# Hybrid decoder trunk on one core: final norm rebuilt on token rows, and four reordered waits

## The reference

```python
for i in range(DEPTH):                      # i = 0: rglru, i = 1: mlstm
    xn = rms_norm(x, norm_mix[i])
    y, *states = mixer(xn, ...)
    x = x + y
    x = x + swiglu(rms_norm(x, norm_ffn[i]), ffn_w_up[i], ffn_w_down[i])
    gate = jax.nn.sigmoid(x @ ple_w_gate[i] + ple_b_gate[i])
    x = x + gate * (p[i] @ ple_w_proj[i])
y = rms_norm(x, norm_final)                 # returned with all new states
```

## Time and profile before

| | |
|---|---|
| three runs, median | 1933.7 us (1928.45, 1933.7, 1937.48) |
| the profiled execution | 1932.01 us, its span 1930.3 us |
| mean granted TensorE clock | 0.991 |
| PE / ACT / DVE / POOL busy | 98% / 38% / 39% / 40% of the span |

### The profile page before, as it was taken

The page is one execution under the profiler, slowest core; times in us unless marked ns, Lnnn a source line. Parts: engine busy times, 40 slices in busy tenths (PEclk is TensorE's granted clock), DMA queues, the critical chain, the costliest instruction groups (busy, mean ns, idle before and its releaser), DMA issues.

```text
span 1930.3 us, 35958 instructions
## 1 busy us (share of the span) xinstructions
PE 1886.2 (98%) x13703; PEld 1751.1 (91%) x13703; DVE 745.5 (39%) x868; ACT 724.4 (38%) x1062; POOL 780.7 (40%) x663
## 2 busy tenths in 40 slices
PE   7999999999999999999999999999999999999997
PEld 7999999999999999998555555999999999999997
DVE  6677632111111122597766667122231111101214
ACT  4576733322222234444433342423443322212342
POOL 3233554444554544464110101544535545545441
PEclk9999999999999999999999999999999999999998
DMA  4222232222222222322489778232322222222222
GB/s 127 82 83 79 86 100 72 82 88 82 82 82 82 82 82 78 94 77 88 160 262 303 238 246 293 77 93 66 97 79 82 82 82 82 82 82 76 88 80 68
DMA packets 187147, 209.70 MB, mean 109 GB/s; under 512 B 24475, under 2 KB 150051, under 8 KB 186991
## 3 DMA queue, kind: packets, MB, share of 16 engines
q1 hardware_dynamic: 186818, 208.19, 34.9%
q10 hardware_dynamic: 224, 0.07, 0.0%
HBM read 167.57 MB, written 40.64 MB: 108 GB/s over the span
## 4 chain that ended last, share of the span: by engine, by line
PE 87%; DVE 4%; issue 4%; DMA 2%; POOL 2%; ACT 2%; SPq 0%; DVEq 0%; POOLq 0%; ACTq 0%
PE ps L2207 73%; PE ps L2455 2%; PE ps L2553 2%; PE ps L2516 2%; POOL W_LO L662 1%; PE ps L2494 1%; DMA out_ml_C_s_dram<-C_HALVES 1%; PE ps L2389 1%; PE ps L2504 1%; PE ps L2573 1%; DVE H_PAD L1687 1%; PE ps L2378 0%; PE ps L2449 0%; DMA X_ROWS<-in_x_prompt_dram 0%; PE ps L2400 0%
## 5 line engine op out<-in xcount | busy, mean ns | idle before, releaser
L662 POOL TENSOR_TENSOR W_LO<-W_RAW,W_HI 128x512 fp32r<-128x512 f32 x464 | 628.6, 1364 | 731.4 <-ACT W_HI L963 663.8
L963 ACT ACTIVATE W_HI<-W_RAW 128x512 fp32r<-128x512 f32 x484 | 298.5, 628 | 711.6 <-PE ps L2207 707.4
L2207 PE MATMUL ps<-A_HI,W_HI 128*128 128x288 f32 x2304 | 496.3, 297 | 13.1 <-DVE A_LO L1522 4.8
L2207 PE MATMUL ps<-A_LO,W_HI 128*128 128x288 f32 x2304 | 494.7, 296 | 0.0
L2207 PE MATMUL ps<-A_HI,W_LO 128*128 128x288 f32 x2304 | 494.5, 296 | 0.0
L2207 PEld LDWEIGHTS ps<-A_HI,W_HI 128*128 128x128 f32 x2304 | 372.3, 189 | 15.4 <-issue 13.2
L2207 PEld LDWEIGHTS ps<-A_LO,W_HI 128*128 128x128 f32 x2304 | 372.7, 189 | 0.0
L2207 PEld LDWEIGHTS ps<-A_HI,W_LO 128*128 128x128 f32 x2304 | 372.6, 189 | 0.0
L1769 DVE TENSOR_TENSOR X<-X,ps 128x1152 f32 (+1 forms) x36 | 48.7, 1354 | 312.4 <-PE ps L2207 312.4
L2207 PE MATMUL ps<-G_HI,W_HI 128*128 128x288 f32 x768 | 164.6, 296 | 0.5 <-DVEq L1795 0.5
L2207 PE MATMUL ps<-G_HI,W_LO 128*128 128x288 f32 x768 | 164.5, 296 | 0.0
(11 more groups left out here) (383 smaller groups left out, 2248.2 us busy)
## 6 DMA issues: line engine op xcount, KB each, us to landing
W_RAW<-in_ffn_w_up_dram SPq DMA_DIRECT2D x176, 256.0 KB, 2.8
C_HALVES<-in_state_mlstm_C_dram SPq DMA_DIRECT2D x64, 512.0 KB, 5.0
out_ml_C_s_dram<-C_HALVES SPq DMA_DIRECT2D x64, 512.0 KB, 5.3
W_RAW<-in_ffn_w_down_dram SPq DMA_DIRECT2D x88, 256.0 KB, 2.6
W_RAW<-in_ml_w_in_dram SPq DMA_DIRECT2D x64, 256.0 KB, 2.8
W_RAW<-in_rg_w_in_dram SPq DMA_DIRECT2D x48, 256.0 KB, 2.7
W_RAW<-in_ple_w_gate_dram SPq DMA_DIRECT2D x32, 256.0 KB, 2.6
W_RAW<-in_ml_w_out_dram SPq DMA_DIRECT2D x32, 256.0 KB, 2.8
```

The lines of the kernel that those rows point to most:

```text
L662: pool.tensor_tensor(W_LO[:, s], W_RAW[:, s], W_HI[:, s].bitcast(F32), ALU.subtract).then_inc(lo_ready, 1)
L963: act.activation(W_HI[:, s], W_RAW[:, s], ACT.Copy).then_inc(hi_ready, 1)
L2207: ins = pe.matmul(ps[:, 4 * s + 2 * m + h, 0:HALF_T], a[:, w, k, wc], x[:, h * HALF_T:h * HALF_T + HALF_T], start=i == 0 and k == 0 and q ...
```

## The change

1. DVE makes the first two low splits of block 1 ahead of the lambda polynomial.
2. In the first PLE, ACT makes three W_HI splits, the gate, then the fourth split.
3. In the first slab behind the heads, PE runs the passes with W_HI for the whole slab (16 matmuls) once W_HI is there, then waits for W_LO and runs the other 8 (`hi_first`).
4. `states()` puts the two N transposes with the 12 of the RG states into set 0 (bank 3), so two copies-out and two frees are left of four.
5. The end. X_GAIN and the sums of squares over features go. X of the first six chunks is turned into token rows between slabs 0, 1 and 2 of the last job (16 + 14 transposes, banks 4 to 7); DVE multiplies them with a gain row into Y_ROWS, and ACT squares them with a sum along the row. Behind the last slab, chunk 7 comes as X and as gate product, both turned by matmuls with the identity that add up in PSUM, and chunk 6 by transposes; five sums on ACT, a total, root and reciprocal, then DVE and ACT scale Y_ROWS in place (DVE tiles 1, 3 and halves of 0 and 4; ACT tile 2 and the other halves), and SP stores each tile when it is ready. Y_ROWS has a place for each of the five tiles.
6. SP loads the gain row, broadcast to 128 partitions (512 KB), behind the P rows of layer 1; the gain's small load at the start goes.

```diff
@@ sync: behind load_p(1, ...)
+            for half in range(2):
+                sp.wait_ge(cp_stored[half], 16 * HEADS)
+            sp.dma_start(GAIN_ROW[:, :], I["norm_final"].rearrange("(o d) -> o d", o=1).broadcast_to([P, D_MODEL])).then_inc(gain_loaded, 16)
             ffn(1)
...
-                sp.wait_ge(out_rows, i + 1)
+                sp.wait_ge(y_tile[i], 2 if i in (0, 4) else 1)
@@ scalar: ple
-                        for k in range(4):
+                        for k in range(3):
                             split_hi()
                         act.wait_ge(slab_used, jobs.adv(4) + 2 * RING)
...
+                            ins = gate(s, c, C_PB + 2 * m + c + 4 * j)
                         ins.then_inc(psum_freed[s], 1)
...
+                        split_hi()
+                        prep(4 * j + 2 * m, gain, dst)
@@ scalar: last_ple
+            def tile_sum(piece, i, src):
+                n, k = TOKEN_TILES[i][1], sums_t.adv()
+                if k > 2:
+                    act.wait_ge(tile_sums, k - 2)
+                act.activation(SQUARES[0:n, k % 2, 0:src.shape[-1]], src, ACT.Square, accum_out=ROW_SUMS[0:n, piece, i:i + 1]).then_inc(tile_sums, 1)
...
+                    if m == 3:
+                        for i in range(4):
+                            act.wait_ge(gained, i + 1)
+                            tile_sum(0, i, ps[:, 4 + i, :])
+                        act.wait_ge(gained, 5)
+                        tile_sum(0, 4, ps[0:N_STOK, 4, :])
+                        for i, (t0, n) in enumerate(TOKEN_TILES):
+                            act.wait_ge(gained, 6 + i // 2)
+                            tile_sum(1, i, ps[0:n, 5 + i // 2, i % 2 * 2 * P:i % 2 * 2 * P + 2 * P])
+                    act.wait_ge(slab_used, jobs.adv(4) + 2 * RING)
...
+                act.activation(RSTD_COLS[:, 7:8], EPS_COL[:, :], ACT.Sqrt)
+                for i, (t0, n) in enumerate(TOKEN_TILES):
+                    act.wait_ge(turned, 3 + i)
+                    tile_sum(2, i, ps[0:n, LAST_BANKS[i], 0:2 * P])
+                act.wait_ge(total_ready, 1)
+                act.activation(RSTD_COLS[:, 0:5], ROW_TOTAL, ACT.Sqrt, bias=EPS_COL[:, :], scale=1.0 / D_MODEL).then_inc(last_root, 1)
+                act.wait_ge(last_rstd, 1)
+                for i, c0 in ((0, 4 * P), (2, 0), (4, 4 * P)):
+                    n = TOKEN_TILES[i][1]
+                    act.wait_ge(gained, 9 + i)
+                    act.activation(Y_ROWS[0:n, i, c0:], Y_ROWS[0:n, i, c0:], ACT.Copy, scale=RSTD_COLS[0:n, i:i + 1]).then_inc(y_tile[i], 1)
@@ vector
             rg_xc_lo(0)
+            rg_lo(1, 0)
+            rg_lo(1, 1)
             dve.wait_ge(lam_e, 1)
...
-            rg_lo(1, 0)
-            rg_lo(1, 1)
             rg_gate(0, 8)
@@ vector: last_ple, behind the gate of the last pair
+                dve.wait_ge(last_gate, 1)
+                link(dve.tensor_tensor(GATE[:, 0, :], GATE[:, 0, :], P_PROJ[:, 6, :], ALU.mult))
+                dve.wait_ge(last_gate, 2)
+                dve.tensor_tensor(GATE[:, 1, :], GATE[:, 1, :], P_PROJ[:, 7, :], ALU.mult).then_inc(last_gated, 1)
+                dve.tensor_tensor(X[:, 6, :], X[:, 6, :], GATE[:, 0, :], ALU.add).then_inc(xf_ready, 1)
...
+                def late_gain(i):
+                    n = TOKEN_TILES[i][1]
+                    dve.wait_ge(tile_sums, 11 + i)
+                    dve.tensor_tensor(Y_ROWS[0:n, i, EARLY:], ps[0:n, LAST_BANKS[i], 0:2 * P], GAIN_ROW[0:n, EARLY:], ALU.mult).then_inc(gained, 1)
+                for i in range(4):
+                    late_gain(i)
+                dve.wait_ge(tile_sums, 15)
+                dve.tensor_tensor(ROW_TOTAL, ROW_TOTAL, ROW_SUMS[:, 2, :], ALU.add).then_inc(total_ready, 1)
+                late_gain(4)
+                dve.wait_ge(last_root, 1)
+                dve.reciprocal(RSTD_COLS[:, 0:5], RSTD_COLS[:, 0:5]).then_inc(last_rstd, 1)
+                dve.wait_ge(last_rstd, 1)
+                dve.wait_ge(gained, 13)
+                for i, c1 in ((0, 4 * P), (1, 8 * P), (3, 8 * P), (4, 4 * P)):
+                    n = TOKEN_TILES[i][1]
+                    dve.tensor_scalar(Y_ROWS[0:n, i, 0:c1], Y_ROWS[0:n, i, 0:c1], RSTD_COLS[0:n, i:i + 1], None, ALU.mult).then_inc(y_tile[i], 1)
@@ tensor: job
+                    if hi_first and i == 0:
+                        n = slabs.adv()
+                        pe.wait_ge(hi_ready, n + DVE_SLABS)
+                        for part in range(2):
+                            if part:
+                                pe.wait_ge(lo_ready, n + RING)
+                            for k, m, h in itertools.product(range(2), range(2), range(2)):
...
+                                if part:
+                                    ins = pe.matmul(dst, W_LO[:, w, k, wc], hi[:, tokens], start=False, stop=False)
+                                else:
+                                    pe.matmul(dst, W_HI[:, w, k, wc], hi[:, tokens], start=k == 0, stop=False)
+                                    pe.matmul(dst, W_HI[:, w, k, wc], lo[:, tokens], start=False, stop=False)
@@ tensor: states
                 use(0)
...
+                pe.transpose(ps[:, 3, 0:P], N_SAMPLES[:, :, :, :].rearrange("p b h k -> p (b h k)"), IDENT[:, :])
+                pe.transpose(ps[0:16, 3, P:2 * P], N_PROMPT[:, :, :].rearrange("p h k -> p (h k)"), IDENT[:, :]).then_inc(misc_done, 1)
                 use(1)
@@ tensor: last_ple
+                def between(i):
+                    if i == 1:
+                        use(1)
+                        pe.wait_ge(xf_ready, 2)
+                        for t in range(4):
+                            for c in range(4):
+                                ins = turn_out(t, c, 4 + t, c * P)
+                        ins.then_inc(turned, 1)
+                    if i == 2:
+                        pe.wait_ge(xf_ready, 3)
+                        pe.wait_ge(tile_sums, 1)
+                        for c in range(4):
+                            turn_out(4, c, 4, c * P)
+                        for t in range(5):
+                            if t % 2 == 0:
+                                pe.wait_ge(tile_sums, 2 + t // 2)
+                            for c in range(2):
+                                ins = turn_out(t, 4 + c, 5 + t // 2, t % 2 * 2 * P + c * P)
+                        ins.then_inc(turned, 1)
+                job(0, 4, chunks(hi, lo), between)
...
+                pe.wait_ge(tile_sums, 10)
+                pe.wait_ge(gained, 8)
+                for i in range(5):
+                    if i == 4:
+                        pe.wait_ge(last_gate, 1)
+                    add_columns(i, X[:, 7, :], True)
+                pe.wait_ge(last_gated, 1)
+                for i in range(5):
+                    add_columns(i, GATE[:, 1, :], False)
+                pe.wait_ge(xf_ready, 4)
+                for i in range(5):
+                    turn_out(i, 6, LAST_BANKS[i], 0).then_inc(turned, 1)
```

More of the change, by code:

```diff
@@ L786, in ple, with last_ple @@
                 next_norm()
-                for j in (range(2) if last else (None,)):
-                    if last:
-                        body(j)
-                    else:
-                        with loop(pool, 2, {slabs: 8}) as j:
-                            body(j)
+                with loop(pool, 2, {slabs: 8}) as j:
+                    body(j)
+            def last_ple():
+                for k in range(4 + 16):
+                    split_lo()
             def body(j):
@@ L2185, in use, with job @@
                     pe.wait_ge(psum_freed[s], before)
-            def job(s, pairs, operand, before=None, first=0, last=None, own=False):
+            def job(s, pairs, operand, before=None, first=0, last=None, own=False, hi_first=False):
                 if first == 0:
@@ L2311, in ffn @@
                     y_done[0] += ks
-            def turn_out(i):
-                (t0, n), s = TOKEN_TILES[i], i % 2
-                use(s)
-                for c in range(CX):
-                    ins = pe.transpose(ps[0:n, 4 * s + c // 4, (c % 4) * P:(c % 4) * P + P], X_GAIN[:, c, t0:t0 + n], IDENT[:, :])
-                ins.then_inc(misc_done, 1)
             def turn_in(layer):
@@ new lines, in last_ple, with add_columns @@
+            def last_ple(P_HI, P_LO, hi, lo, xn0):
+                project(1, P_HI, P_LO)
+                for m in range(3):
+                    job((m + 1) % 2, 4, chunks(hi, lo), lambda i: pe.wait_ge(xn_ready, xn0 + i + 1))
+                def between(i):
[14 more added lines that the diff above has]
+                                pe.wait_ge(tile_sums, 2 + t // 2)
+                            for c in range(2):
+                                ins = turn_out(t, 4 + c, 5 + t // 2, t % 2 * 2 * P + c * P)
+                        ins.then_inc(turned, 1)
+                job(0, 4, chunks(hi, lo), between)
+                def add_columns(i, src, first):
+                    t0, n = TOKEN_TILES[i]
```

(3 more changed lines are left out.)

214 lines of the change are left out of this document (106 added, 108 removed).

## The result

| | before | after |
|---|---|---|
| median, runs on the same chip | 1934.8 us (10 runs, 1928.45 to 1939.18) | 1917.5 us (10 runs, 1915.48 to 1922.8) |
| ratio, 95% interval | | 0.9915, 0.9901 to 0.9928 |
| profiled execution, its span | 1932.0, 1930.3 us | 1917.9, 1916.2 us |
| mean granted clock | 0.991 | 0.994 |

The kernel became faster by 0.85%. The two traces are 14.1 us apart, the medians 17.4.

The account below looks back on a forecast made before the run. TensorE, busy 98% of the span, was taken as the bound. Gains 2.3 + 0.5 + 3.3 + 2.25 + 4.7 = 13.05 us gave 1918.9 for the profiled execution, 1920.6 against the median; range 1914 to 1927.

Parts of the forecast that it names:

- clock behind the gate: Behind the first PLE's gate, granted clock 0.57 over 4 us; its return, 1.7 us, counted only in a rival of chance 0.16.
- Part 1: Near 50 us, two low splits ahead of the lambda chain end PE's wait: gain 2.3 us, range 1.3 to 2.3.
- Part 2: First PLE: the gate ahead of the fourth W_HI split starts 0.54 us earlier; gain 0.5, range 0 to 0.6.
- Part 3: First slab after the heads: high passes first gain 1.6 us, returned clock 1.74; together 3.3, range 1.0 to 3.3.
- Part 4: State transposes: four small sets in one less two hand-offs; gain 2.25 us, range 1.8 to 2.6.
- Part 5: Kernel end: transposes in the last job's stream, shorter chain, stores at 373 GB/s; gain 4.7 us, bounds 0.9 to 7.9.
- the table load: At the end, the root's table load takes 1.28 us beside DVE and PE; with the skill's drain 2.66, end gain 4.5.
- Part 6: Gain row's load in SP's queue ahead of the FFN slabs: cost 0, with 8.8 us to spare.
- More comes out: Rival: lower clock behind the first PLE also goes (1.7), stores overlap better (3.2): 18.0 us, time 1915.7; chance 0.16.
- The waits only move: Rival: PE arrives earlier, next splits or copies are late, two gains lose 2 each: 9 us, time 1924.7; chance 0.10.
- Less comes out: Rival: lower clock stays behind the heads, stores and dear transposes hold the end: 8.2 us, time 1925.5; chance 0.20.

Follow-up runs that it names:

- part 2 undone: The changed kernel with four W_HI splits ahead of the gate again in the first PLE; median 1919.1 us, ratio 0.9923 to the kernel before.
- part 3 undone: The changed kernel with the first slab behind the heads in its old matmul order; median 1920.6 us, ratio 0.9926 to the kernel before.
- part 4 undone: The changed kernel with four small sets of state transposes instead of two; median 1921.3 us, ratio 0.9941 to the kernel before.

## Why the prediction was right, point by point

The median is 1917.5, the prediction said 1920.6; for the profiled execution it said 1918.9 and 1917.9 was measured. In differences the forecast was 13.1, the spans gave 14.1 and the medians 17.4. The 1.0 in the spans is close partly by luck: 1.5 of clock behind the gate that the sum left out stood against 1.1 lost at the start and in the heads, which no part of the change explains. The table has the steps of the sum, in us of the traces.

| step | predicted | measured | by |
|---|---|---|---|
| 1 lambda | 2.3 | 1.9 (the wait: 2.3) | marks |
| 2 gate | 0.5 | 0.35 | marks; part 2 undone |
| clock behind the gate | rival only | 1.5 | marks 791 to 802, part 2 undone |
| 3 high passes first, with the clock | 3.3 | 3.0 | part 3 undone |
| 4 states | 2.25 | 2.65 | part 4 undone |
| 5 end | 4.7 | 5.7 | two traces with the new end |
| 6 gain row | 0 | 0 | no wait of PE |
| start of the span, and the heads | 0 | -1.1 | marks |
| sum | 13.05 | 14.0 (by the spans: 14.1) | |

**Part 1** was right in the wait, which went whole, and in its cover: PE has no wait at the third slab, and DVE is full (3.81 of 4 us from 52). **Part 2** was mis-sized: the 0.54 between split and gate does not come back whole, as the gate starts 0.30 behind PE's release, where the split ahead of it had started 0.12 behind. Inside the loop something stands there that the profile does not show. Written out, the wait is 1.46, near the 2.07 - 0.54 = 1.53 that the step wanted.

**Part 3.** PE began at 1195.70, 0.63 behind the heads (0.5 was said), the low part came in time, the second slab waited 0.3 (0.4 was said). The clock came back here in this trace, and in 7 of 11. The step took it as returned because the stand is short; 4 of 11 traces show that a stand of 0.6 does not exclude a fall. What the prediction drew from the Trainium skill (TensorE: Matmul & The Clock Gate, "Part 1: The HAM clock gate"), that the clock gate samples on its own beat, fits the runs, which do not show it: the same place with the same stand had both outcomes, four times one and seven times the other.

**Part 4** gave 0.4 more: the first N copy started 1.67 behind the start of the RG_ROWS copy where 2.06 was taken, and the two N copies took 0.47 together and not 0.6. Some 0.14 went the other way, as DVE began the RG_ROWS copy 1.73 behind the first transpose and not 1.59.

**Part 5** was right in its order and in what ends it, and its marks hold, counted from the end of the last slab (E, 1900.37): the product of chunk 7 and the sum of chunk 6 are done at E+3.0 (2.9 was said), the first tile at E+4.2 (3.85), the last sum of squares at E+6.1 (6.5), the reciprocal at E+6.9 (7.3), the first store at E+7.7 (8.0), the end at E+15.8 (16.5). Three terms make the 1.0 that came on top. The transposes in the stream took 3.3 and not 3.6. The chain up to the first store was 0.3 shorter, by two errors against each other. The first tile came 0.37 later than said, although the matmuls ran at full clock: the five matmuls of the gate product are ten rows and took 1.45 up to the first transpose, where 5 x 0.246 was said. The five sums of squares then followed each other every 0.36, where 0.5 was said, and took 1.9 in all instead of 2.6. And behind the first store 0.4 went: 2.01 MB passed from 1909 to 1914, that is 402 GB/s and not 373. The row of the 373 has a DMA share of 0.92, so it was not a full stretch; 373 / 0.92 = 405. In the last microsecond, with the sample rows, 254 GB/s passed at a share of 1.02.

On the table load the measurement decides against the rule that the prediction named (the Trainium skill, ScalarE: Activation LUTs, "What ACT_TABLE_LOAD costs"): the load starts at 1901.78 and the next ACTIVATE at 1903.08, 1.30 behind it. There was no drain on top that the row shows. The first sum of squares did start at E+4.2, which is the figure that the rule gave, but for another reason: ACT stood 1.31 there for PE's transposes.

**Part 6** was right in its cost of nothing, with the wrong slack: 10.9, not 8.8.

**The rivals.** "More comes out" wanted the clock behind the first PLE and stores that overlap better. The first came, with 1.5 of its 1.7; of the 3.2 for the stores 0.4 came. The median of 1917.5 lies between the forecast and this rival, 1920.6 and 1915.7, but most of that distance is in where the medians stand and not in these two terms. "The waits only move" did not happen: behind parts 1, 2 and 4 no wait grew. The new waits are the 0.63 ahead of the first high pass, 0.3 for the low part behind it, and 1.15 for the gate product at the end, all inside the terms of the sum. "Less comes out" failed in both of its conditions here, though its first, the clock behind the heads, is true in 4 of 11 traces. The failing step in the size is one: the prediction asked for the clock behind the heads alone whether it comes back, took that behind the gate as a rival, and none behind the lambda chain, where it had seen 1.00 in the one trace. One trace shows one outcome of such a place.

## What to carry to other kernels

When the busiest engine is at 98%, list its waits and cost each one by the chain that ends it, then add to each stand, a short one too, a possible fall of TensorE's clock behind it; a single trace shows one outcome, so count it over several before taking it as there or not there. At the end of a kernel, move what can be computed early into the stream of the last job, also when it costs the busy engine the same time there, because what is saved is the waiting around it (8.1 us here); and then count the bytes of the last stores, as they set the end once the compute is short.
